# Rotation of q and k: the swap of neighbouring channels by transfers inside SBUF in place of a permutation product

## What is computed

```python
h = rms_norm(x, mix_pre_g[l]) * (1.0 + scale1) + shift1
z = h @ w_in[l]
q = z[..., :o1].reshape(B, S, N_Q_HEADS, HEAD_DIM)
k = z[..., o1:o2].reshape(B, S, N_KV_HEADS, HEAD_DIM)
q = apply_rope(rms_norm(q, q_norm_g[l]), cos, sin)
k = apply_rope(rms_norm(k, k_norm_g[l]), cos, sin)

def apply_rope(x, cos, sin):
    xf = x.astype(jnp.float32).reshape(*x.shape[:-1], HEAD_DIM // 2, 2)
    x0, x1 = xf[..., 0], xf[..., 1]
    out = jnp.stack([x0 * c - x1 * s, x0 * s + x1 * c], axis=-1).reshape(x.shape)
```

## Time and profile before

| | us |
|---|---|
| median of 3 runs | 3502.03 |
| lowest, highest run | 3496.61, 3503.22 |
| the profiled execution, its own time | 3501.04 |
| its span, first to last instruction | 3499.2 |
| PE busy in the span | 3226.1 (92%) |
| DVE busy | 2469.2 (71%) |
| ACT busy | 1184.0 (34%) |
| POOL busy | 261.6 (7%) |

### The profile page before, as it was taken

The page is one execution under the profiler, slowest core; times in us unless marked ns, Lnnn a source line. Parts: engine busy times, 40 slices in busy tenths (PEclk is TensorE's granted clock), DMA queues, the critical chain, the costliest instruction groups (busy, mean ns, idle before and its releaser), DMA issues. The chain is left out here.

```text
span 3499.2 us, 35353 instructions
## 1 busy us (share of the span) xinstructions
PE 3226.1 (92%) x13985; PEld 2554.7 (73%) x13985; DVE 2469.2 (71%) x2707; ACT 1184.0 (34%) x1512; POOL 261.6 (7%) x323
## 2 busy tenths in 40 slices
PE   3789999998699999968999989999997999999996
PEld 3667766666577777747777878888886788888884
DVE  7539676675288888866666467776675777777777
ACT  4113211110388899852323232222222322222122
POOL 2001504421000000000000000000000100000002
PEclk7899999999799999989999999999999999999998
DMA  5642312221711211136675522112214311111113
GB/s 193 210 153 90 133 72 82 102 88 61 233 41 33 52 34 34 34 80 212 210 222 194 216 89 59 45 54 59 59 59 151 110 59 40 59 40 59 47 52 116
DMA packets 134741, 344.14 MB, mean 98 GB/s; under 512 B 26504, under 2 KB 35720, under 8 KB 130088
## 3 DMA queue, kind: packets, MB, share of 16 engines
q1 hardware_dynamic: 117552, 302.03, 27.4%
q10 hardware_dynamic: 11520, 20.98, 1.6%
q0 software_dynamic: 5504, 18.88, 1.4%
HBM read 249.64 MB, written 92.19 MB: 98 GB/s over the span
## 5 line engine op out<-in xcount | busy, mean ns | idle before, releaser
L1974 DVE TENSOR_TENSOR second_y<-second_y,second_ps_b 128x512 f32<-128x512 f32 x672 | 456.2, 687 | 221.1 <-PE second_ps_b L92 221.1
L90 PE MATMUL second_ps_a<-second_h_hi,up_wu_hi 128*128 128x512 f32 x1408 | 551.8, 392 | 27.6 <-DMA second_h_lo<-scratch_h 17.6
L91 PE MATMUL second_ps_a<-second_h_lo,up_wu_hi 128*128 128x512 f32 x1408 | 550.9, 391 | 0.0
L92 PE MATMUL second_ps_a<-second_h_hi,up_wu_lo 128*128 128x512 f32 x1408 | 550.5, 391 | 0.0
L1181 DVE TENSOR_TENSOR att_prob_lo<-att_prob,att_prob_hi 128x1024 fp32r<-128x1024 f32 x256 | 307.5, 1222 | 66.2 <-ACT att_prob_hi L1156 65.3
L90 PEld LDWEIGHTS second_ps_a<-second_h_hi,up_wu_hi 128*128 128x128 f32 x1408 | 266.2, 189 | 84.7 <-issue 18.0
L90 PE MATMUL proj_ps<-h_hi,proj_w_hi 128*128 128x512 f32 x704 | 299.3, 425 | 9.1 <-DVE proj_w_lo L719 9.1
L92 PEld LDWEIGHTS second_ps_a<-second_h_hi,up_wu_lo 128*128 128x128 f32 x1408 | 266.3, 189 | 55.7
L91 PEld LDWEIGHTS second_ps_a<-second_h_lo,up_wu_hi 128*128 128x128 f32 x1408 | 266.3, 189 | 55.4
L90 PE MATMUL second_ps_b<-ffn_wd_hi,ffn_g_hi 128*128 128x512 f32 x704 | 277.1, 394 | 26.2 <-DVE second_y L1974 13.7
L1150 ACT ACTIVATE att_prob<-att_ps_s 128x1024 f32<-128x1024 f32 x256 | 263.9, 1031 | 58.6 <-PE att_ps_s L1224 58.6
(11 more groups left out here) (219 smaller groups left out, 5788.0 us busy)
## 6 DMA issues: line engine op xcount, KB each, us to landing
up_w_st<-in_w_up SPq DMA_DIRECT2D x88, 512.0 KB, 5.9
ffn_wd_st<-in_w_dn SPq DMA_DIRECT2D x44, 512.0 KB, 3.6
fin_ada_w<-in_w_ada SPq DMA_DIRECT2D x32, 512.0 KB, 5.3
scratch_gates<-proj_out SPq DMA_DIRECT2D x64, 256.0 KB, 2.0
merge_w_st<-in_w_branch SPq DMA_DIRECT2D x32, 512.0 KB, 6.2
merge_gate<-scratch_gates SPq DMA_DIRECT2D x64, 256.0 KB, 3.0
scratch_h<-merge_x ACTq DMA_DIRECT2D x48, 256.0 KB, 5.4
proj_w_st<-in_w_z SPq DMA_DIRECT2D x22, 512.0 KB, 4.0
```

The lines of the kernel that those rows point to most:

```text
L90: pe.matmul(out, w_hi, x_hi, start=first, stop=False)
L91: pe.matmul(out, w_hi, x_lo, start=False, stop=False)
L92: return pe.matmul(out, w_lo, x_hi, start=False, stop=last)
L1974: dve.tensor_tensor(at, at, ps_d[:, q % 4, :], ALU.add).then_inc(s_y, 1)
```

## The change

The product with the permutation matrix goes, and with it the matrix as an input and its load. In its place SP waits for step i's copy and square and issues two DMA transfers from `zg` to `rot`, both in SBUF: one writes the even partitions from the odd ones, the other the odd from the even, 64 rows of 512 values (128 KB) each. DVE multiplies `rot` by the sines in place when both have landed (32 on a semaphore, one semaphore for each of the two buffers), and does not wait for PE's mean product there any more. SP's loop over the loads of weights is written out, with the transfers of a chunk's four steps behind that chunk's load. ACT and POOL keep their streams. The core of the diff:

```diff
@@ -449,7 +449,7 @@
         bg = r.sb("bg", [P, 2 * KD])
         gains = r.sb("gains", [P, NQC + 1])
         small = r.sb("small", [P, 4, P])
-        swap, head_mean, mx, mx2 = (small[:, i, :] for i in range(4))
+        head_mean, mx, mx2 = (small[:, i, :] for i in range(1, 4))
         eps = r.sb("eps", [P, 1])
         hi_st = r.sb("hi_st", [P, NB, BLK], F32R)
         v_hl = r.sb("v_hl", [P, NKV, BLK], F32R)
@@ -466,7 +466,8 @@
         s_c, s_eps = r.sem("consts"), r.sem("eps_written")
         s_w = [r.sem(f"w_loaded{i}") for i in range(2)]
         s_hi, s_lo, s_mm, s_zg, s_ms, s_std, s_rot, s_out, s_rope = (
-            r.sem(n) for n in ("w_hi_made", "w_lo_made", "products", "zg_sq", "mean_swap", "root", "rotated", "v_or_gate", "rope"))
+            r.sem(n) for n in ("w_hi_made", "w_lo_made", "products", "zg_sq", "mean", "root", "rotated", "v_or_gate", "rope"))
+        s_sw = [r.sem(f"pairs_swapped{i}") for i in range(2)]
         s_rhi, s_rlo = r.sem("rotated_hi"), r.sem("rotated_lo")
         s_f, s_dft, s_z, s_zst = (r.sem(n) for n in ("f_loaded", "dft_steps", "z_split", "z_stored"))
         s_tr, s_v, s_vst = r.sem("v_turned"), r.sem("v_split"), r.sem("v_stored")
@@ -492,14 +493,22 @@
                                  w_z[bass.ds(c, 1), :, :].rearrange("o p (k m) -> p o k m", k=KD)).then_inc(s_w[u], 16)
                 load(0, 0)
-                for dst, src in ((cos, rope_cos), (sin, rope_sin), (bg[:], b_gate), (gains[:], qk_g), (swap, swap_d),
+                for dst, src in ((cos, rope_cos), (sin, rope_sin), (bg[:], b_gate), (gains[:], qk_g),
                                  (head_mean, head_mean_d)):
                     sp.dma_start(dst, src).then_inc(s_c, 16)
                 load(1, 1)
-                with sp.Fori(0, NQKV // 2) as i:
-                    for u in range(2):
-                        sp.wait_ge(s_lo, 2 * i + u + 1)
-                        load(2 * i + u + 2, u)
+
+                def swap_pairs(i):
+                    sp.wait_ge(s_zg, i + 1)
+                    for a in range(2):
+                        sp.dma_start(rot[a:P:2, i % 2, :], zg[1 - a:P:2, i % 2, :]).then_inc(s_sw[i % 2], 16)
+
+                for c in range(NQKV):
+                    sp.wait_ge(s_lo, c + 1)
+                    load(c + 2, c % 2)
+                    if c <= NQC:
+                        for n in range(NB):
+                            swap_pairs(NB * c + n)
                 def load_f(g):
                     sp.dma_start(z, f_d.rearrange("t p c -> p t c")[:, :, g * P:(g + 1) * P]).then_inc(s_f, 16)
@@ -725,15 +734,16 @@
                 dve.memset(eps[:], EPS).then_inc(s_eps, 1)
                 lo_part(0, 0)
-                dve.wait_ge(s_c, 16 * 6)
+                dve.wait_ge(s_c, 16 * 5)
                 for c in range(NQC + 1):
                     lo_part(c + 1, (c + 1) % 2)
                     for n in range(NB):
                         cols = slice(n * BLK, (n + 1) * BLK)
-                        done = 4 * (4 * c + n)
+                        i = 4 * c + n
+                        done = 4 * i
                         zc, rc, sc = zg[:, n % 2, :], rot[:, n % 2, :], std[:, n % 2, :]
-                        dve.wait_ge(s_ms, 4 * c + n + 1)
-                        dve.tensor_tensor(rc, ps_sw[:, n % 2, :], sin[:, cols], ALU.mult).then_inc(s_rope, 1)
+                        dve.wait_ge(s_sw[n % 2], 32 * (i // 2 + 1))
+                        dve.tensor_tensor(rc, rc, sin[:, cols], ALU.mult).then_inc(s_rope, 1)
                         dve.tensor_tensor(zc, zc, cos[:, cols], ALU.mult).then_inc(s_rope, 1)
                         dve.wait_ge(s_rope, done + 2)
                         dve.tensor_tensor(rc, rc, zc, ALU.add).then_inc(s_rope, 1)
@@ -800,11 +810,10 @@
                 def rope_products(c, n):
                     if c == 0 and n == 0:
-                        pe.wait_ge(s_c, 16 * 6)
+                        pe.wait_ge(s_c, 16 * 5)
                     pe.wait_ge(s_zg, 4 * c + n + 1)
                     if c or n >= 2:
                         pe.wait_ge(s_rot, 4 * c + n - 1)
-                    pe.matmul(ps_sw[:, n % 2, :], swap, zg[:, n % 2, :], start=True, stop=True)
                     pe.matmul(ps_ms[:, n % 2, :], head_mean, sq[:, n % 2, :], start=True, stop=True).then_inc(s_ms, 1)
                 for c in range(NQC + 2):
...
@@ -2202,11 +2211,9 @@
     ang = np.concatenate([(t // grid_w)[None, :] * inv[:, None], (t % grid_w)[None, :] * inv[:, None]])
     ang = np.tile(np.repeat(ang, 2, axis=0), (2, 1))
     sign = np.where(np.arange(P) % 2 == 0, -1.0, 1.0)[:, None]
-    swap = np.zeros((P, P))
-    swap[np.arange(P) ^ 1, np.arange(P)] = 1.0
     head_mean = np.kron(np.eye(2), np.full((HD, HD), 1.0 / HD))
     made = {"t_pos": pos.transpose(1, 0, 2, 3).reshape(P, K1, 3 * P), "t_chan": chan.reshape(P, 3 * P), "rope_cos": np.cos(ang),
-            "rope_sin": sign * np.sin(ang), "swap": swap, "head_mean": head_mean, "ident_d": np.eye(P)}
+            "rope_sin": sign * np.sin(ang), "head_mean": head_mean, "ident_d": np.eye(P)}
     return {k: np.ascontiguousarray(v.astype(np.float32)) for k, v in made.items()}
```

More of the change, by code:

```diff
@@ L423, in _, with proj_phase @@
                     m.then_inc(s_mm, 1)
-def proj_phase(nc, w_z, hT_hi, hT_lo, b_gate, qk_g, rope_cos, rope_sin, swap_d, head_mean_d, ident, f_d, qk_d, gates_d,
+def proj_phase(nc, w_z, hT_hi, hT_lo, b_gate, qk_g, rope_cos, rope_sin, head_mean_d, ident, f_d, qk_d, gates_d,
                z_d, v_d, m_d):
@@ L673, in _ @@
                 hi_part(0, 0, 0)
-                act.wait_ge(s_c, 16 * 6)
+                act.wait_ge(s_c, 16 * 5)
                 act.wait_ge(s_eps, 1)
@@ L2140, in program @@
 def program(nc, x, c, w_ada, b_cols, b_ada, pre_g, post_g, w_f, w_z, b_gate, qk_g, w_branch, w_out, w_up, conv, w_dn,
-            t_pos, t_chan, rope_cos, rope_sin, swap, head_mean, ident_d, out, scratch_kind="Internal"):
+            t_pos, t_chan, rope_cos, rope_sin, head_mean, ident_d, out, scratch_kind="Internal"):
     def scratch(name, shape, dt=F32):
@@ L2174, in program @@
             f_phase(nc, w_f, h_hi, h_lo, f_d, make_ada(3, 3, 4, 2, 5))
-            kept = proj_phase(nc, w_z, h_hi, h_lo, b_gate, qk_g, rope_cos, rope_sin, swap, head_mean, ident, f_d,
+            kept = proj_phase(nc, w_z, h_hi, h_lo, b_gate, qk_g, rope_cos, rope_sin, head_mean, ident, f_d,
                               qk_d, gates_d, z_d, v_d, m_d)
```

## The result

| | before | changed |
|---|---|---|
| median of 6 runs, us | 3499.32 | 3475.13 |
| lowest, highest | 3495.29, 3504.09 | 3467.16, 3476.16 |
| the profiled execution, its span | 3501.04, 3499.2 | 3476.16, 3474.3 |

The changed kernel takes 0.9925 of the time before (95% interval 0.9912 to 0.9939): 24.2 us less. Lines of `kernel.py` are 9 or 10 further down in what follows: L736, L737, L739, L741, L747 are now L746, L747, L749, L751, L757; L684, L685, L671, L667 are L693, L694, L680, L676; L808 is L817.

What follows compares the result with a forecast made beforehand. PE, busy 92% of the span, bounds the kernel; after the change DVE and ACT pace the q and k steps. 11.4 us plus 0.86 of the last swap give 12.2 us: 3502.0 - 12.2 = 3489.8 us, range 3481 to 3502.

Steps and rivals of the forecast that it cites:

- What bounds: In the q and k steps, DVE and ACT, not PE, set the new pace: 27.68 us per chunk against 28.84 before.
- the ring: Two-buffer `zg` loop through ACT's copy and root and DVE's reciprocal to L747: 6.95 us per step, hidden before by PE's 7.21.
- Start: First q and k steps: L747 of step 0 at 243.6 us, of step 1 at 250.9 us.
- The sum in the stage, 12.2: PE's product of step 19 at 363.7 instead of 375.09 us, 11.4 gained, plus 0.86 of the last swap: 12.2 us.
- Transfers: SBUF transfers of q and k steps land in 0.1 + 0.93 + 2.7 = 3.7 us, 1.9 inside the cover, costing nothing.
- (1): ACT's ring does not hold in the q and k steps; PE's 6.35 rules, full 17.2 us gained, 3484.8; chance 0.10.
- (2): Transfer halves land one after the other: 2.4 us less gain, 3492; with 7 us of landing 3496 to 3502, chance 0.05.
- (3): Slower: transfers landing later than 6.75 us, each further us costing 0.5 us per step; 3572 at 14.1 us; chance 0.08.
- (4): Gain handed back in the next chunk, where ACT's fourth v copy waits for a store; 3502; chance 0.07.
- I found no later work that is tied to anything but the end of the one before it: What PE gains in the q and k stage travels through the gate stage and all later work.
- the full 17.2: Most the change can give: 20 swap products of 0.86 us removed from PE's queue in the q and k steps.
- the cover: Time SP's transfers may take before DVE's L736 needs them: 5.6 us, 0.6 more before the reciprocal is late.

Runs made afterwards that it cites:

- root_first: Changed kernel with ACT's root of step i-1 placed ahead of the high part of step i-2; stage 622.5 us, median 3477.36 us, ratio to before 0.9945.
- product_kept_in_half: Changed kernel with an unread permutation product made by PE in two steps of four; stage 629.9 us, median 3488.04 us, ratio to before 0.9971.
- B: The kernel before the change; median 3499.32 us at first, 3498.60 us when run again unchanged, ratio 1.0004, stage 640.0 and 640.1 us.
- A: The changed kernel, measured four times; medians 3475.13, 3479.17, 3477.16 and 3472.65 us, ratios to before 0.9925, 0.9946, 0.9946 and 0.9920.

## Why the prediction was wrong, and where it was right

- **What bounds, and the ring.** Right. Steps in a chunk are 7.46, 6.89, 6.89 and 6.33 where 7.46, 6.95, 6.95 and 6.32 were forecast, a chunk 27.6 against 27.68. (That PE's small products would stand 6.9 us apart on average doesn't follow from the prediction's own times: 363.7 less 238.16 over 19 steps is 6.6, because PE is ahead at first, and 6.6 is what they show.) `root_first` showed by intervention that ACT's order is in the path, and `product_kept_in_half` that PE has room: 8.6 us of its work cost 3.1.
- **Start.** Right within 0.5 us. Both profiles must be laid on each other at the first small product, from which the prediction counts: it stands at 234.8 and not at 238.16, 3.3 us earlier (the stage starts 4.2 earlier, but its first blocks run 1 us longer at the half clock). With this shift L747 of step 1 stands at 250.8 (forecast 250.9) and the product of step 19 at 363.2 (forecast 363.7). The first transpose of v comes 16.0 us earlier in the profile, 12.7 after the shift, where 12.2 were forecast.
- **The sum in the stage, 12.2.** It was 13.2: 12.7 up to the first transpose of v, 1.4 behind it, and 1.0 lost again to the slower start. The gates I took to be moved as they are; the waits of PE for DVE's maxima there were 2.6 us in 7 waits and are 1.3 us in 6. Before, from 376 us on:

```profile
PE proj_ps_sw L845 <- DVE proj_small L771: 1.7, 6, 0.6
PE proj_ps_ms L845 <- DVE proj_small L771: 0.9, 1, 0.9
```

  After, from 361 us on:

```profile
PE proj_ps_sw L854 <- DVE proj_small L781: 1.3, 6, 0.2
```

  But the second profile of B has the short waits too, from 376 us on:

```profile
PE proj_ps_sw L845 <- DVE proj_small L771: 1.2, 6, 0.2
```

  So the 1.3 us are within B's own scatter, and nothing shows them to be the change's. Counted from the first small product the stage is 626.2 to 627.5 us in the five profiles of B's kind and 613.3 to 613.5 in the seven of A's, 12.7 to 14.3 apart: 12.2 was short by 0.5 to 2. That the pair of profiles gave 13.2 is in part luck.
- **Transfers.** They cost nothing, as forecast. Landing 2.1 us where 2.7 was taken from the stores, and from square to both landed 2.6 in the median (4.0 at most) against 3.7. Here the prediction's sum counts the second issue twice: a landing runs from the start of its own issue, so only the first issue of the pair (0.53 us) comes on top of it. The Trainium skill (DMA: Bandwidth & Descriptors, Anatomy of one DMA — SWDGE (gpsimd) path) gave an estimate of 2.3 us for the landing; it is a fit for transfers that GpSimd issues, and the 2.1 of these, which SyncE issues, is near it.
- **Rivals.** (1) fell: DVE's own 6.32 and the ring stand above PE's 6.35 in each chunk. (2) fell: a pair has landed 2.6 us after its first issue, and 3.9 where the second half is issued only when the first has landed, so the halves overlap. The rule of that page (Rules for kernel authors) that two disjoint halves serialize isn't borne out by these 128 KB transfers, and even in turn they cost nothing. (3) is true as a mechanism, with the right price per step, and didn't apply. (4) fell: ACT's v copy waited 5.6 us at most for a store and PE for nothing behind it.
- **The step that failed** is the sentence "I found no later work that is tied to anything but the end of the one before it", by which all that comes after the stage was moved one for one, and the range's lower end, which allowed 3 or 4 us for scatter beyond the full 17.2. In the first measurement the time came 14.7 us below the forecast's 3489.8. Of these, 2.7 are the base (the forecast started from 3502.0, the median of three runs; that of six is 3499.3), 1.0 is the stage, and 11.0 are outside it, a term that the prediction had at nothing. Outside the stage this change was measured at -11.0, -4.4, -5.5 and -13.2 us. Taking 8.5, their mean, as its size, 13.2 + 8.5 = 21.7 is the gain, 3476 for B at 3497.7. What makes it wasn't found and stays open; the profile pair puts 4.2 of 11 ahead of the stage, and this part is within the scatter.

## What to carry to other kernels

When two or three engines are nearly full, write down each ring between buffers term by term from one step's rows: it gave the new pace here to 0.06 us, while "PE saves 17.2" was off by 4. A latency that sits on a two-buffer ring costs nothing up to the cover; beyond it the ring gives the price, and that was right here once the latency was read from the trace. So work out the cover first (here 5.6 us, against 2.6 needed) before fearing or trusting a transfer. Lay two profiles on each other at the work that changed, not at the start of the stage. And before a few tenths of a per cent are explained, run both kernels again: the stage repeated to about 1 us, the gain of the whole only to 9 us in four measurements on different chips, so a range for a total needs that scatter and not that of three runs.

## What I had not expected of the hardware

- A transfer of 128 KB inside SBUF, 64 odd partitions from 64 even ones, lands in 2.1 us (median of 40; 1.9 to 3.5), where 256 KB stores to memory in the same stage take 2.6 and 2.9, and its issue takes SP 0.57 us. In the run with four per step, one after the other, the median is 2.0.
- The two halves of a pair overlap: both have landed 2.6 us after the first issue, 3.9 when the second waits for the first.
- The same code varies very differently by place: what lies ahead of the stage ended between 219.5 and 229.1 us in 17 profiles, while the stage from its first small product on took 613.3 to 613.5 us in the seven profiles of A's kind.
- The granted clock alone moves the stage by 1 us from one profile to the next: it stays at half for about 3 us after the stage's first product in some (0.61 or 0.62 over the first 4 us) and for 5 in others (0.50, then 0.87).
